# A decoder block with 32 experts on one core: last batch in quarter pieces, another way from the output projection to the experts

## The reference

```python
merged = sigmoid(gate_a) * (y_a @ w_nsa_up) + sigmoid(gate_r) * (y_r @ w_ret_up)
x = x + merged @ w_out
h = rmsnorm(x, norm_ffn)
# hierarchical_moe(h):
lg = h @ w_rg + b_rg                       # 4 groups
p_grp, grp = top_k(softmax(lg), 1)
le = (h @ w_re + b_re).reshape(B, S, 4, 8) # 32 experts
top_l, top_i = top_k(le[..., grp, :], 2)
w_sel = softmax(top_l) * p_grp
combine = sum over the two of one_hot(grp * 8 + top_i, 32) * w_sel
for each expert (wg, wu: 1024x256, wd: 256x1024, c = its column of combine):
    out += (silu(h @ wg) * (h @ wu)) @ wd * c
return rmsnorm(x + out, norm_final)
```

## Time and profile before

| | us |
|---|---|
| median of 3 runs | 487.83 (485.97 to 489.0) |
| the profiled execution | 485.28 |
| its span in the trace | 483.6 |
| TensorE busy | 440.7 (91%) |
| VectorE busy | 191.7 (40%) |
| ScalarE busy | 79.1 (16%) |
| GpSimd busy | 23.9 (5%) |
| moved by DMA | 150.76 MB, mean 312 GB/s |

### The profile page before, as it was taken

How to read it: one execution, slowest core, us unless ns; L and a number is a source line. 1 busy time by engine, 2 the same in 40 slices (tenths; PEclk the granted TensorE clock), 3 DMA queues, 4 the chain that set the end, 5 groups by cost and what they waited for, 6 DMA issues and landing times.

```text
span 483.6 us, 5717 instructions
## 1 busy us (share of the span) xinstructions
PE 440.7 (91%) x2242; PEld 230.7 (48%) x2242; DVE 191.7 (40%) x435; ACT 79.1 (16%) x213; POOL 23.9 (5%) x44
## 2 busy tenths in 40 slices
PE   9999999999999999999999989999995876849952
PEld 5599744555555555454444865355351422304210
DVE  1563128827955768788631353121020100101003
ACT  1000122313243011110002341011010100101021
POOL 2020000310000010000002110000000000000001
PEclk9999999999999999999999999999997798988998
DMA  8999638409208008959996499999999999999972
GB/s 253 429 421 375 213 124 344 178 12 400 111 0 348 0 0 327 403 205 431 398 362 263 175 362 403 415 432 432 416 431 430 424 427 421 433 426 430 423 304 90
DMA packets 24810, 150.76 MB, mean 312 GB/s; under 512 B 5420, under 2 KB 7885, under 8 KB 18254
## 3 DMA queue, kind: packets, MB, share of 16 engines
q1 hardware_dynamic: 19440, 147.36, 74.5%
q10 hardware_dynamic: 5342, 3.00, 2.0%
HBM read 147.73 MB, written 2.62 MB: 311 GB/s over the span
## 4 chain that ended last, share of the span: by engine, by line
PE 72%; DMA 12%; SPq 10%; DVE 3%; issue 2%; ACT 0%; POOLq 0%; DVEq 0%; POOL 0%; ACTq 0%
PE bank L700 31%; PE bank L675 30%; SPq L472 8%; DMA ring<-in_moe_gate_up 6%; PE bank L1125 5%; DMA qkT<-in_moe_down 4%; PE bank L1102 3%; PE bank L706 2%; SPq L469 2%; DMA ring<-in_dense 1%; DVE ring L1655 0%; DVE nsa L1564 0%; DVE hT_and_y L2113 0%; DVE nsa L2042 0%; SPq L453 0%
## 5 line engine op out<-in xcount | busy, mean ns | idle before, releaser
L700 PE MATMUL bank<-ring,x 128*128 128x512 f32 x128 | 57.3, 594 | 0.0
L675 PE MATMUL bank<-ring,nsa 128*32 128x512 f32 x304 | 41.1, 679 | 17.0 <-DMA ring<-in_moe_gate_up 14.3
L2051 DVE SCALAR_TENSOR_TENSOR wr<-cst,bank 128x256 f32<-128x256 f32 x8 | 3.4, 421 | 112.0 <-ACT cst L1505 112.0
L700 PE MATMUL bank<-ring,hT_and_y 128*128 128x512 f32 x96 | 43.4, 597 | 0.0
L700 PEld LDWEIGHTS bank<-ring,x 128*128 128x128 f32 x128 | 23.8, 190 | 27.6 <-issue 27.5
L1125 PEld LDWEIGHTS bank<-selection,Tb 128*128 128x128 f32 x256 | 30.4, 195 | 8.7 <-issue 8.7
L1125 PE MATMUL bank<-selection,Tb 128*128 128x128 f32 x256 | 32.6, 281 | 1.1 <-issue 0.7
L675 PEld LDWEIGHTS bank<-ring,nsa 128*32 128x32 f32 x304 | 9.6, 117 | 46.0 <-issue 24.2
L1102 PE MATMUL bank<-nsa,selection 128*128 128x512 f32 x64 | 29.8, 606 | 1.7 <-DVE nsa L2042 0.9
L2042 DVE COPY nsa<-bank 128x512 f32<-128x512 f32 x16 | 11.1, 692 | 49.4 <-PE bank L675 28.0
L675 PE MATMUL bank<-hT_and_y,ring 128*128 128x256 f32 x128 | 28.2, 380 | 0.1
(11 more groups left out here) (259 smaller groups left out, 638.4 us busy)
## 6 DMA issues: line engine op xcount, KB each, us to landing
ring<-in_moe_gate_up SPq DMA_DIRECT2D x19, 2048.0 KB, 21.7
ring<-in_dense SPq DMA_DIRECT2D x17, 2048.0 KB, 9.2
hT_and_y<-in_moe_gate_up SPq DMA_DIRECT2D x5, 2048.0 KB, 22.4
spare<-in_moe_gate_up SPq DMA_DIRECT2D x4, 2048.0 KB, 23.4
vr_and_gr<-in_moe_gate_up SPq DMA_DIRECT2D x4, 2048.0 KB, 23.8
nsa<-in_moe_down SPq DMA_DIRECT2D x11, 512.0 KB, 18.1
windows<-in_moe_down SPq DMA_DIRECT2D x7, 512.0 KB, 16.6
qkT<-in_moe_down SPq DMA_DIRECT2D x7, 512.0 KB, 17.4
```

Source lines behind the costliest of these rows:

```text
L675: return nc.tensor.matmul(o, l, r, start=s, stop=e)
L700: ins = nc.tensor.matmul(o, l[:, k, :], r[:, k, :], start=first and k == 0, stop=last and k == n - 1, skip_group_check=True)
L2051: V.scalar_tensor_tensor(hid_e, th_sb, 1.0, bank[k][:, 0:FF], ALU.add, ALU.mult).then_inc(s_hch, 1)
```

## The change

It has five parts.

**1. Loads.** The right half of the output weights is laid out in SBUF as two blocks of 256 columns, so out3 uses the lower half of its home and out4 the upper. Piece 5 is loaded in two halves of 1 MB: the first when out3 is done, the second when out4 is. Piece 7 is loaded in two halves, the first when the first k step of piece 0 is used. The last piece (31) comes in halves with a semaphore each.

**2. Router.** Group and expert logits swap places, so that one operation scales both. The index is compared as it is, without a cast to float, and both experts' one-hots come from one operation into `onehot`; TensorE takes the places from these two (two products), while VectorE adds them to `comb1`. Transposes x2T12 stand ahead of the route steps 4 and 5.

**3. Gather of batch 0.** Its first four k tiles are in two banks, F0 (bank 2) and G0; the filler matmuls are gone and the counts come behind the gather.

**4. Last batch.** The down weights of the last four experts are laid out by quarters of the columns: each load of 512 KB holds one k step (f) of one quarter (256 columns) for all four experts. Down runs by quarters O0 to O3, each with its copy on VectorE (before: two halves, the left on ScalarE), and its sums of 256 columns.

**5. End.** The number of rounds is read ahead of the last batch. GpSimd takes one power for both tiles; ScalarE scales and stores both left halves, VectorE scales both right halves, which SyncE stores.

```diff
@@ SyncE: loads
             sp.wait_ge(*is_full("out2"))
             first_gu(4)
+            sp.wait_ge(*is_full("out3"))
+            gu_half(5, 0)
             sp.wait_ge(*is_full("out4"))
-            first_gu(5)
+            gu_half(5, 1)
             first_dw(9, (0,))
...
             def reload_gu(e):
+                if e == NGU:
+                    sp.wait_ge(s_half_used, 1)
+                    gu_half(e, 0)
+                    sp.wait_ge(*piece_used(0, 0, 0))
+                    gu_half(e, 1)
+                    return
@@ VectorE: router(t)
-                link(V.scalar_tensor_tensor(rt[:, t, 40:44], o[:, 0:NG], st[:, 36 + t:37 + t], rbias[:, 0:NG], ALU.mult, ALU.add))
-                freed(f"route{t}", V.scalar_tensor_tensor(rt[:, t, 4:36], o[:, NG:NG + NE], st[:, 36 + t:37 + t],
-                                                          rbias[:, NG:NG + NE], ALU.mult, ALU.add))
+                freed(f"route{t}", V.scalar_tensor_tensor(rt[:, t, 8:44], o[:, 0:NE + NG], st[:, 36 + t:37 + t], rbias[:, :], ALU.mult, ALU.add))
+                dve.wait_ge(*is_emptied(f"route{t}"))
                 V.max(rt[:, t, 48:56], rt[:, t, 40:48]).then_inc(s_rm, 1)
                 dve.wait_ge(s_rm, 2 * t + 1)
                 link(V.max_index(ri[:, t, 0:8], rt[:, t, 48:56], rt[:, t, 40:48]))
-                link(V.tensor_copy(rt[:, t, 104:105], ri[:, t, 0:1]))
-                link(tsc(rt[:, t, 60:64], iota[:, 0:NG], rt[:, t, 104:105], NEG, ALU.not_equal, ALU.mult))
-                dve.wait_ge(*is_emptied(f"route{t}"))
-                link(V.tensor_tensor(masked, le, rt[:, t, 60:64].unsqueeze(2).broadcast_to((P, NG, EPG)), ALU.add))
+                link(V.tensor_tensor(rt[:, t, 60:64], iota[:, 0:NG], ri[:, t, 0:1].broadcast_to((P, NG)), ALU.not_equal))
+                link(V.scalar_tensor_tensor(masked, rt[:, t, 60:64].unsqueeze(2).broadcast_to((P, NG, EPG)), NEG, le, ALU.mult, ALU.add))
                 V.max(rt[:, t, 96:104], rt[:, t, 64:96]).then_inc(s_rm, 1)
                 dve.wait_ge(s_rm, 2 * t + 2)
                 link(V.max_index(ri[:, t, 8:16], rt[:, t, 96:104], rt[:, t, 64:96]))
-                link(V.tensor_copy(rt[:, t, 104:106], ri[:, t, 8:10]))
-                link(tsc(rt[:, t, 124:156], iota, rt[:, t, 104:105], None, ALU.is_equal, ALU.bypass))
-                V.scalar_tensor_tensor(comb1[:, t, :], iota, rt[:, t, 105:106], rt[:, t, 124:156], ALU.is_equal, ALU.add).then_inc(s_M, 1)
+                V.tensor_tensor(onehot[:, t, :, :], iota.unsqueeze(1).broadcast_to((P, 2, NE)),
+                                ri[:, t, 8:10].unsqueeze(2).broadcast_to((P, 2, NE)), ALU.is_equal).then_inc(s_M, 1)
                 dve.wait_ge(s_M, t + 1)
+                V.tensor_tensor(comb1[:, t, :], onehot[:, t, 0, :], onehot[:, t, 1, :], ALU.add).then_inc(s_member, 1)
@@ TensorE: last batch
-                down(0)
                 out("WT.c")
-                out("O0.c")
-                final_sum(0, 0)
-                final_sum(1, 0)
-                down(1)
-                out("O1.c")
-                final_sum(0, 1)
-                final_sum(1, 1)
+                final_sums(0)
+                final_sums(1)
+                down_quarter(2)
+                o3 = start("O3.c")
+                down_piece(3, 0, o3)
+                final_sums(2)
+                down_piece(3, 1, o3)
+                final_sums(3)
+                def final_sums(q):
+                    w = slice(q % 2 * 256, q % 2 * 256 + 256)
+                    out(f"O{q}.c")
+                    for t in range(TT):
+                        ins = nc.tensor.matmul(bank[4 + 2 * t + q // 2][:, w], selWT[:, t * P:(t + 1) * P], o_sb[:, q // 2, w],
+                                               start=False, stop=True, skip_group_check=True)
+                        if q % 2:
+                            ins.then_inc(s_sum, 1)
@@ ScalarE: end
-            act.wait_ge(s_rstd, 9)
-            nc.scalar.activation(final[:, 1, 0:512], final[:, 1, 0:512], ACT.Copy, scale=st[:, 39:40]).then_inc(s_fq, 1)
+            act.wait_ge(s_rstd, 8)
+            for t in range(TT):
+                nc.scalar.activation(final[:, t, 0:512], final[:, t, 0:512], ACT.Copy, scale=st[:, 38 + t:39 + t]).then_inc(s_fq, 1)
+            for t in range(TT):
+                act.wait_ge(s_fq, t + 1)
+                act.dma_start(out[0, t * P:(t + 1) * P, 0:512], final[:, t, 0:512]).then_inc(s_out, 16)
```

More of the change, by code:

```diff
@@ L126 @@
 SUMMED = ((0, 0), (1, 0), (0, 1), (1, 1))
-SEG = dict(first=GATHER_N, body=BATCH_C + GATHER_N + DOWN_C, last=FINAL_C + BATCH_C + DOWN_C)
+SEG = dict(first=GATHER_N, body=BATCH_C + GATHER_N + DOWN_C, last=FINAL_C + BATCH_C + [f"O{q}.c" for q in range(4)])
 SEG_BANK0 = dict(first=len(BATCH_C) % 4, body=0, last=0)
@@ L400, in loads_before, with extra_loads @@
             return len(range(home, NE, homes)) + (r - 1) * NB
+        def extra_loads(home, later):
+            return 1 if home == 5 or home == 0 and later else 0
         def place(seg, job, r, b=0):
@@ L1254, in one_round @@
                         steps("body", r, b, weights(b))
-                else:
-                    with pe.Fori(0, NB - 1) as b:
-                        steps("body", r, b, weights(b))
+                    left = rounds_left(pe)
+                    steps("last", r, 0, weights(NB - 1))
+                    return left
+                with pe.Fori(0, NB - 1) as b:
+                    steps("body", r, b, weights(b))
                 steps("last", r, 0, weights(NB - 1))
@@ L1526, in one_round @@
                         steps("body", r, b)
-                else:
-                    with act.Fori(0, NB - 1) as b:
-                        steps("body", r, b)
+                    left = rounds_left(act)
+                    steps("last", r, 0)
+                    return left
+                with act.Fori(0, NB - 1) as b:
+                    steps("body", r, b)
                 steps("last", r, 0)
-                if not isinstance(r, int):
-                    act.wait_ge(s_sum, r * 4 + 4)
-                    nc.scalar.activation(st[:, 223:224], ident[:, 0:1], ACT.Copy)
+                act.wait_ge(s_sum, r * 4 + 4)
+                nc.scalar.activation(st[:, 223:224], ident[:, 0:1], ACT.Copy)
             rounds(act, one_round)
```

219 lines of the change are left out of this document (141 added, 78 removed).

## The result

The changed kernel takes 481.76 us (median of 4 runs, 481.66 to 483.28), the kernel before 487.88 (4 runs, 485.97 to 489.0): ratio 0.989, with a 95% interval from 0.986 to 0.993. The forecast was 483.4. Its profiled execution took 481.76 us with a span of 480.0, where before it was 485.28 and 483.6: 3.5 us less. The execution profiled before was faster than each of its four runs; the one after lies at its median, so the medians lie further apart than the two traces.

What follows compares the result with a forecast made beforehand. The expert-weight DMA stream was taken to bound the kernel. Gains of 2.4 us from earlier loads and 2.0 us after the last landing, 4.4 us off the median of 487.83, gave 483.4 us, range 480.8 to 486.5.

Steps and rivals of the forecast that it cites:

- What bounds the kernel: Whole kernel: the expert-weight stream, not TensorE, sets the pace; only earlier DMA idle time, bytes and the end work matter.
- The rival of a start for each added load: Three added loads each pay a restart of 1.3 us though the queue is full: 487.3 us, chance 0.02.
- Part 2, the router to piece 7: Batch start: shorter routing starts the first gate/up step 1.1 us earlier, so piece 7's load goes out before the queue empties.
- Part 1, the early half: Loads near 275 us: half of piece 5 issued after out3 fills the DMA hole, gaining 2.4 us.
- the rival of the gap not filled: Piece 5's first half starts late or slowly, so the stream gains only 1.1 us: 484.7 us, chance 0.16.
- Part 3, the tail: After the last landing: quarter pieces shorten matmuls, copy, sums and power, less a scaling loss; 2.0 us gained.
- It fits with 0.6 to spare: Before the last landing: TensorE's 4.3 us of work fits the 4.9 us since the left half's fourth landing.
- the two signs that I had named for being wrong: Last landing unmoved though the gap is filled, or TensorE still on sums when the last piece lands.
- The scaling with the stores: Kernel end: ScalarE scaling two halves loses 0.72 us, issuing its own store gains 0.35; net loss 0.35.
- The clock in the tail: TensorE's clock falls near the end: whole tail 488.5 us, chance 0.04; short dip (484.8) or fall at 283 (485.8), 0.10.
- the rival in which stream and tail gain all they can: Loads gain 2.9 us and the work after the last landing 2.5: 482.4 us, chance 0.13.
- Taking the difference off the median: Whole kernel: the 4.4 us gain was subtracted from the shown median 487.83, which was 2.5 above the profiled execution.

Runs made afterwards that it cites:

- sums behind: The changed kernel with the third quarter's sums on TensorE moved after both halves of the fourth quarter; 481.47 and 481.33 us, ratios 0.987 and 0.988 to the kernel before.

## Why the prediction was right, and where its terms were off

**What bounds the kernel**: right. The long stretch runs as before, 424 GB/s at a share of 1.01, and the gain came ahead of it and behind it:

```profile
293.00:467.00 174.00, 149.16 (x1048) 63.42 (x1044) 22.48 (x58) 18.64 (x43) 0.00 (x0) 0.92 1.01 424
```

The rival of a start for each added load (487.3) fell with this row and with the filled hole. The Trainium skill (DMA: Bandwidth & Descriptors, "Anatomy of one DMA — SWDGE (gpsimd) path") counts about 2 us as fixed in every DMA, measured on another path; the estimate from it in the prediction, 489.4, is 7.6 us above the measured time. A load into a queue that is almost empty loses somewhat less than that here (the two large dips lack 0.66 and 0.48 MB, 1.6 and 1.1 us at 424 GB/s), and one in a full queue shows no loss (419 GB/s behind piece 7 in the run without the early half).

**Part 2, the router to piece 7**: right step by step. Membership at 282.48 (forecast 282.6), places at 282.62 (282.65), their result at 283.56 (283.5), first gate/up piece at 287.02 (287.0), piece 7 at 288.15 (288.1). The sentence behind it was wrong: "its data can flow at 288.6, before the queue empties at 289.1". It was issued in time and data did flow, but the rate was at 188 and 270 GB/s until 291.

**Part 1, the early half**: it went out at 274.20 (274.16), the second half at 278.27 (278.05). Whether the full 2.4 us was too much depends on the measure: 1.8 to 2.0 by the bytes in nine profiles, between the forecast and the rival of the gap not filled (1.1); 2.7 on average by the last landing, where 468.5 was forecast and the nine average 468.4. One term is wrong by either measure, the cost of a late issue: I took 0.1 us for the second half, as if a queue with a little left lost nothing. The dip from 278 to 281 lacks 0.66 MB against 424 GB/s, the one from 288 to 291 0.48 MB. The row that should have warned me was in the earlier trace rows: 342 instead of 426 after the hole. I priced this ramp as a rival only for the case that the gap is not filled; it stands behind each of the three issues into a queue with little left, smallest behind the first (279 GB/s for 2 us, 0.29 MB, issued 1.3 us ahead). With 1 MB more in the queue, the same issue of piece 7 made no dip (419 GB/s in the run without the early half).

**Part 3, the tail**: 1.7 us instead of 2.0 by the span. Matmuls 1.37 (1.35 forecast), copy 0.26 (0.27), sums 0.43 (0.43), squares and power 0.55 (0.35). "It fits with 0.6 to spare" failed, and with it came one of the two signs that I had named for being wrong: TensorE still worked on sums when the last piece landed. The last piece waited 0.5 us, 0.4 more than before. I had compared totals over five pieces, 4.3 against 4.9 us, where only the last gap counts: the piece before is used from 467.88, as it lands, the last one lands 1.1 us later, and between them stand half a quarter (0.57 to the next start) and the sums (1.06), 1.6 us. The scaling with the stores was mis-sized: a loss of 0.35 was forecast; it was 1.2 to the end of the last issue and 0.5 to the end of the span. In this stretch a single issue on ScalarE's queue takes 1.4 us, which in other profiles of the same stores took 0.36 to 2.0; the span hardly follows it.

**The clock in the tail**: I gave it 0.04 for the whole tail and 0.10 for a short dip. The low clock stood in 5 of the 10 profiles that have the new tail without fillers, for 3.4 to 6.8 us, and in neither of the two with the old one. It starts between 459.9 and 462.5, in or behind waits of 1.1 to 1.9 us in the last batch; the five profiles without it have waits of 1.1 to 1.8 us. Without it the last piece starts 0.5 to 0.6 us late in the order of the changed kernel, with it 1.0 to 2.5. So the chance of a dip was far too small, while the case that I priced at 5.05 us, the whole tail, never came: in all five the clock is back, at 467.2 at the latest, before TensorE starts on the last piece. It never cost the gain.

**The sum**: 2.4 + 2.0 = 4.4 was forecast, 1.9 + 1.7 = 3.6 stands in the two profiles, and the medians lie 6.1 and 4.9 apart (two groups of runs). The measured 481.76 is inside the range of 480.8 to 486.5, but 1.6 us below the forecast, below the forecast's own range (482.3 to 484.5), and nearest to the rival in which stream and tail gain all they can (482.4). The traces don't bear that rival's mechanism out: the dips were there and the tail gained 1.7, not 2.5. That the measured time came out this low is chance in part, not a step that the prediction had foreseen. Taking the difference off the median was right in kind; that the measured one is larger than the profiles' I put down to the scatter of the runs, which is not shown: those of before lie between 484.2 and 490.0 (29 of them), those of the changed kernel between 481.5 and 483.3. Why the kernel before scatters more wasn't found.

**A version ahead of both**: sums behind, 481.3 to 481.5 us, 1.2 to 1.3% below the kernel before. Against the changed kernel it is ahead by less than can be told.

## To carry to other kernels

When a queue bounds the kernel, count the bytes over the whole stretch from the first hole to where the queue is full for good: an edit that fills one hole may only move it (piece 4 in halves, or, for the most part, the early half or the router by itself), and what pays in full is the pair that closes both ends. Issue a load well before the queue runs out: here one issued 1.3 us ahead still had a small dip, two with less left had larger ones, and one with 1 MB (2.5 us) more in the queue none. Where between these the dip ends was not measured. Near the end of a kernel, price the order of the engine's own work at the last landing with measured durations of the same shape, and expect nothing from issue order or early stores below the scatter of the last store's landing.

## What the runs showed that I had not expected

- After an issue into a nearly empty queue the rate took 2.5 to 3 us to come back (156, 188, 270, 401 GB/s in slices of 1 us), though data never stopped altogether.
- The granted clock fell in some executions of a kernel and not in others, with nearly the same waits of 1.1 to 1.4 us: 0.50 from 460 on in the first profile of sums behind, 1.00 in the second.
- One store's issue took 1.41 us on ScalarE's queue in the profile of the changed kernel, 1.44 on SyncE's in the run with all stores there, and 0.36 in others; a store's landing scattered from 3.3 to 5.0 us for the slowest of the last ones.
- The last load landed anywhere between 467.8 and 469.0 us in nine profiles whose loads move nearly the same bytes up to 293 us (339 to 344 GB/s).
